# First taps of a feed-forward unit by seven, queued beside products of the next unit by seven

## What is computed

```python
n2 = _rms(h, norm_ffn_w[l])
up = _causal_dwconv(n2 @ w_up[l], ffn_dw_w[l], ffn_dw_b[l])   # 3 taps over the positions
gate, val = jnp.split(up, 2, axis=-1)                          # 2816 channels each
h = h + (jax.nn.silu(gate) * val) @ w_down[l]
```

## Time and profile before

| | |
|---|---|
| median of 3 runs | 1819.34 us |
| the profiled execution | 1819.85 us |
| its span, first to last instruction | 1818.1 us |
| granted TensorE clock | 0.999 |
| TensorE busy | 1795.2 us (99%) |
| VectorE busy | 1390.7 us (76%) |
| ScalarE busy | 964.0 us (53%) |
| GpSimd busy | 154.3 us (8%) |
| feed-forward part, about | 547 to 908 us of the span |

### The profile page before, as it was taken

One profiled execution on the slowest core, in us unless ns is written; L12 is line 12 of the kernel. 1 busy time (PEld: TensorE's weight loads), 2 busy tenths in 40 slices (PEclk: granted clock), 3 DMA queues, 4 the chain that ended last, 5 costly groups with the idle time before them and its releaser, 6 DMA issues.

```text
span 1818.1 us, 32992 instructions
## 1 busy us (share of the span) xinstructions
PE 1795.2 (99%) x13654; PEld 1711.6 (94%) x13654; DVE 1390.7 (76%) x2436; ACT 964.0 (53%) x1874; POOL 154.3 (8%) x130
## 2 busy tenths in 40 slices
PE   9999999999999999999999999999999999999998
PEld 8999999978899989899899999999899999999987
DVE  5888897678756778857889797978358888787844
ACT  6222333568734446536556665666337566666632
POOL 0000000000000011010002121211000111111000
PEclk9999999999999999999999999999999999999999
DMA  5222222200222166454347776765332677777431
GB/s 196 94 85 78 93 94 70 94 24 27 68 76 93 60 167 144 118 138 109 115 117 149 160 160 149 162 152 131 118 93 76 130 156 156 156 152 158 115 123 70
DMA packets 245444, 210.35 MB, mean 116 GB/s; under 512 B 6454, under 2 KB 241775, under 8 KB 245294
## 3 DMA queue, kind: packets, MB, share of 16 engines
q1 hardware_dynamic: 182974, 177.29, 31.7%
q0 software_dynamic: 62304, 30.94, 13.8%
q10 hardware_dynamic: 16, 0.00, 0.0%
HBM read 206.11 MB, written 2.10 MB: 115 GB/s over the span
## 4 chain that ended last, share of the span: by engine, by line
PE 84%; DVE 8%; ACT 6%; issue 1%; DMA 1%; SPq 0%; DVEq 0%; ACTq 0%
PE ps L195 55%; PE ps L199 27%; DVE wlo L210 2%; PE ps L204 2%; ACT whi L207 1%; ACT p L207 1%; DMA s1t<-in_w_up_dram 1%; ACT y L207 1%; DVE raw L210 1%; DVE ast L1135 0%; DVE y L218 0%; ACT zr L207 0%; ACT sw L207 0%; DVE nf L218 0%; DVE mxl L210 0%
## 5 line engine op out<-in xcount | busy, mean ns | idle before, releaser
L210 DVE TENSOR_TENSOR wlo<-raw,whi 128x1024 fp32r<-128x1024 f32 (+1 forms) x359 | 434.8, 1216 | 207.1 <-ACT whi L207 205.5
L207 ACT ACTIVATE whi<-raw 128x1024 fp32r<-128x1024 f32 (+1 forms) x359 | 376.5, 1051 | 239.5 <-PE ps L195 189.3
L195 PE MATMUL ps<-nhi,whi 128*128 128x256 f32 (+3 forms) x1520 | 341.9, 290 | 2.6 <-DVE clo L210 0.8
L195 PE MATMUL ps<-nhi,wlo 128*128 128x256 f32 (+3 forms) x1520 | 337.9, 287 | 0.0
L195 PE MATMUL ps<-nlo,whi 128*128 128x256 f32 (+2 forms) x1392 | 300.7, 287 | 0.0
L195 PEld LDWEIGHTS ps<-nhi,whi 128*128 128x128 f32 x1520 | 246.8, 189 | 6.7 <-DVE clo L210 1.0
L195 PEld LDWEIGHTS ps<-nhi,wlo 128*128 128x128 f32 x1520 | 246.1, 189 | 2.1
L199 PE MATMUL ps<-thi,whi 128*128 128x256 f32 x784 | 224.8, 287 | 1.4 <-DVE wlo L210 0.8
L195 PEld LDWEIGHTS ps<-nlo,whi 128*128 128x128 f32 x1392 | 221.4, 189 | 1.9
L199 PE MATMUL ps<-thi,wlo 128*128 128x256 f32 x784 | 221.6, 283 | 0.0
L199 PE MATMUL ps<-tlo,whi 128*128 128x256 f32 x784 | 221.4, 282 | 0.0
(11 more groups left out here) (342 smaller groups left out, 3514.3 us busy)
## 6 DMA issues: line engine op xcount, KB each, us to landing
raw<-in_w_in_dram SPq DMA_DIRECT2D x90, 1024.0 KB, 5.8
raw<-in_w_up_dram SPq DMA_DIRECT2D x22, 1024.0 KB, 5.4
raw<-in_w_out_dram SPq DMA_DIRECT2D x20, 1024.0 KB, 5.0
s1t<-in_w_in_dram SPq DMA_DIRECT2D x49, 256.0 KB, 2.8
s1t<-in_w_in_dram POOLq DMA_DIRECT2D x49, 256.0 KB, 7.2
raw<-in_w_in_dram POOLq DMA_DIRECT2D x49, 256.0 KB, 4.7
raw<-in_w_down_dram SPq DMA_DIRECT2D x16, 512.0 KB, 3.4
raw<-in_w_conv_out_dram SPq DMA_DIRECT2D x4, 1024.0 KB, 5.0
```

The costliest lines, as they stand in the source:

```text
L195: return pe.put(after, lambda e: e.matmul(o, w, m, start=start, stop=stop_), mark)
L207: return ac.put(after, lambda e: e.activation(o, i, func, **kw))
L210: return dv.put(after, lambda e: e.tensor_tensor(o, a, b, op))
```

## The change

- `seven` loses its parameter `half`: no first tap is queued ahead of product 7.
- `up_seven` gets a parameter `carry` and puts its two first taps (with the entries in `later` that belong to them) on a list `begins`. If another unit by seven of the same group follows directly, they stay there; otherwise both are queued after hook 6.
- If `begins` holds taps, hook 1 and hook 5 of the next unit by seven queue one each, and `step()` is called at hooks 3 and 6 in place of 2 and 5. Otherwise the steps stay at 2 and 5.
- In `up_taps` for tiles with `scaled[0]`, `step()` comes before the first tap in place of behind it.

```diff
--- before.py
+++ after.py
@@ -561,7 +561,7 @@
             for _ in range(min(n, len(loose))):
                 loose.pop(0)()
 
-        def seven(dst, banks, after, hook, direct, summed_, used, width=256, half=None):
+        def seven(dst, banks, after, hook, direct, summed_, used, width=256):
 
 
             s0 = taken[0]
@@ -612,8 +612,6 @@
             c12 = tt([t, u2], d12, C, d12, ALU.add)
             release(c12, banks[2])
             hook(5)
-            if half:
-                half([c11, c12])
             t = used[3] = product(A, dh[:, :, right], dl[:, :, right], td, summed_(3), False, True, u3)
             done(t, s0 + 3)
             c21 = act([t, c22], d21, A, ACT.Copy, scale=-1.0)
@@ -1469,25 +1467,38 @@
                 up_taps(n, a, j, atok, jl, Y[n], lambda i: ZR[n][:, i:i + T2])
                 loose_run(2 if scaled[0] else 1)
 
-            def up_seven(j, atok, jl, banks):
+            begins = []
+
+            def begin(n=2):
+                for _ in range(min(n, len(begins))):
+                    begins.pop(0)()
+
+            def up_seven(j, atok, jl, banks, carry):
+
 
                 ns = [next_y(), next_y()]
+                begins_due = bool(begins)
 
                 def hook(m):
                     tick(1)
-                    if m in (2, 5):
+                    if m in (1, 5):
+                        begin(1)
+                    if m in ((3, 6) if begins_due else (2, 5)):
                         step()
-
-                def taps_of(c, t):
-                    z = ZR[ns[c]].rearrange("p (h t) -> p h t", h=2)
-                    up_taps(ns[c], t, j + c, atok, jl + c, Y[ns[c]].rearrange("p (h t) -> p h t", h=2), lambda i: z[:, :, i:i + 256], False)
 
                 t = seven([ZR[n] for n in ns], banks, [zr_used[n] for n in ns], hook,
                           lambda r, c: (NHI[:, 4 * r:4 * r + 4, SPAN[c]], NLO[:, 4 * r:4 * r + 4, SPAN[c]], ntok[4 * r:4 * r + 4]),
-                          lambda i: (SHI[i], SLO[i], [stok[i]] * 4), [None] * 4, 258, lambda t: taps_of(0, t))
-                taps_of(1, t[1])
+                          lambda i: (SHI[i], SLO[i], [stok[i]] * 4), [None] * 4, width=258)
+                for c, n in enumerate(ns):
+                    z = ZR[n].rearrange("p (h t) -> p h t", h=2)
+                    begins.append(lambda c=c, n=n, z=z: up_taps(n, t[c], j + c, atok, jl + c, Y[n].rearrange("p (h t) -> p h t", h=2),
+                                                                lambda i: z[:, :, i:i + 256], False))
+                if not carry:
+                    begin()
 
             def up_taps(n, ready_, j, atok, jl, y, z, steps=True):
+                if steps and scaled[0]:
+                    step()
                 b = act([ready_, t_vec, y_used[n]], y, z(0), ACT.Identity, bias=cf[:, 132 + j:133 + j], scale=cf[:, j:j + 1])
 
                 def taps():
@@ -1513,7 +1524,7 @@
                         d = tt([up["h", j]], ALO[:, jl, :], AF[:, jl, :], AHI[:, jl, :].bitcast(F), ALU.subtract)
                         atok[jl] = [up["h", j], d]
 
-                if steps:
+                if steps and not scaled[0]:
                     step()
                 later.append([taps, meet, high, rest])
 
@@ -1637,13 +1648,13 @@
                         zs = two_tiles(([pair_dst(TQ), pair_dst(TQ)], HALVES), NHI, NLO, ntok)
                         ffn_stats()
                     elif j in GATES_BY_SEVEN:
-                        up_seven(2 * j, atok, 2 * (j - ja), [6, 7, 4])
+                        up_seven(2 * j, atok, 2 * (j - ja), [6, 7, 4], j in VALUES_BY_SEVEN)
                     else:
                         for c in range(2):
                             z = tile(TQ, NHI, NLO, ntok)
                             up_out(*z, 2 * j + c, atok, 2 * (j - ja) + c)
                     if j in VALUES_BY_SEVEN:
-                        up_seven(NFF + 2 * j, atok, 2 * (j - ja), [5, 2, 3])
+                        up_seven(NFF + 2 * j, atok, 2 * (j - ja), [5, 2, 3], j + 1 < jb)
                     for c in range(2) if j not in VALUES_BY_SEVEN else ():
                         v = tile(TQ, NHI, NLO, ntok)
                         if j == 0 and c == 0:
```

## The result

The changed kernel takes **1813.41 us** (median of 7 runs, 1812.09 to 1814.40), the kernel before 1819.40 in the same comparison (7 runs, 1819.12 to 1821.83): a ratio of 0.9964, 95% interval 0.9952 to 0.9975, so 6.0 us faster where 5.5 were forecast (1813.8 in 1812.6 to 1816.0). A second comparison on another occasion gave 1813.95 against 1819.53, so 5.6 us, ratio 0.9970 (0.9960 to 0.9981).

A forecast was written before the change was run, and what follows sets the result against it. TensorE, busy 99% of the span, was taken as the bound, so only its idle places could yield time. -6.0 us at five late products and +0.5 at G7 gave -5.5, from 1819.34 to 1813.8 us, range 1812.6 to 1816.0.

The forecast's parts named there:

- five late products: Product 3 in V5, G6, V7, V9 and G10, waiting for ScalarE's copy-out of bank A; 6.0 us with restarts.
- Parts 1 to 3: Five unit boundaries: moving first taps away saves 6.0 us; SiLU entering two boundaries and taps at hooks 1, 5 cost nothing.
- One sign: At unit boundaries, `c21` was to start 0.2 us after product 7 instead of waiting for VectorE.
- Part 4: VectorE in V5 and G6: 20.28 us of work in 20.2; cost 0, bounds 0 and +0.2 per unit pair.
- Part 5: Tile units, step before first tap: one more `ahi` ahead of G7's `s1` costs +0.5 us, bounds 0 and 0.7.
- Part 6: In G7 an `alo` moves ahead of the splits for V7's product 3: cover 0.3 us, cost 0, bound +0.3.
- Part 7: G4, G8 and the ends of V7, G6, G10: taps after the last hook cost nothing, cover several us.
- rival (b): Time given back: TensorE reaches each down stage 2 to 3 us earlier and waits there; about 1819 us, chance 0.06.
- Rival (c): Slower: the first tap at hook 1 waits for VectorE, delaying product 5 at five places; 1823 us, chance 0.05.
- Rival (d): Table change around each SiLU that loses its neighbour: price 0 by rows, 1822 by the skill's 2.7 us each; chance 0.01.

## Why the prediction was right, point by point

*What bounds.* Right: TensorE's five late products were the place, and the gain came from there. Their 5.63 and the 0.4 behind them went entirely.

*Parts 1 to 3.* The sums made from one start to the next held to 0.1: `s1` of G6 at E+1.95 (709.29 less 707.34; forecast 1.94), and product 3 was due 0.42 after its release (forecast 0.43); c0 in V5 at E+4.11 and `u2` at E+4.82 (forecast 4.05 and 4.75). One sign did not come at G7/V7, where `c21` waited for VectorE's `c22` and started at E+0.45, not E+0.20; it cost nothing, since `s1` came at E+1.68, and 1.64 was forecast. The run with both taps at the end shows that queue time and wait are two terms: 0.48 remains at V5 with the wait gone, 0.46 was worked out. That the steps are not what gains is shown by the two runs that take them apart.

*Part 4.* Right to take 0, but by a count that was too high. It laid the 20.28 us of VectorE's work in V5 and G6 against 20.2 of time; in the changed kernel the two units hold 9.61 and 9.02, 18.63 in 20.16, as stages come a step later and fall in part behind G6. The run with added work shows how far it was from a bound: 0.6 more per unit cost 0.3 us in all by the trace (0.21 and a slow restart, at V7).

*Part 5, mis-sized.* "For G5 and G9 the sum before `s1` is the same" was the step that failed. The instructions were the same, but not their sum: 0.15 less at each of G5, G7 and G9, because a tap no longer stands directly behind the copy that it reads; the run with the order alone shows it. G7 therefore came 0.60 late, not 0.75, and G5 and G9 0.08, not 0.23. The direction at G7 was right: the `ahi` that moved there costs its 0.52, and the run that takes a tap from there gets the stop back. With 0.45 more the forecast becomes -5.95; the stretch G5 to G10 shows -6.2 (0.11 of the rest lies between the end of V7 and the start of G8), the medians -6.0. The total came out near because the one mis-sized term is small, and not because two errors met.

*Part 6.* V7's split ended at 742.05 and product 3 was due at 742.50, so 0.45 ahead; the forecast's own times (746.0 and 746.46) give the same. With 0.6 of VectorE's work added, product 3 was 0.21 late and began 0.05 after the split's end. So the release takes 0.05 and the cover was 0.40, where the forecast had 0.3.

*Part 7 and rival (b).* No new stop in the down stages or behind; from the end of G10 to the end of the span both traces take 965.6 us, so nothing is given back.

*Rival (c)* took one microsecond for each microsecond of stop. It did not come: c0 waited for nothing in V5 (701.37, straight behind the split). Whether its price was right no run shows. At its threshold the stops are 1.8 us each; behind those of 1.58 and 2.09 no slow stretch followed, behind those of 2.32 and more one may, and then a stop costs some 1.5 us on top.

*Rival (d).* A SiLU alone between a split and a copy (708.77 to 709.29) takes its 0.52 without idle time. The trace of the changed kernel agrees with the rows of before, and not with a change of tables there.

## What to carry to other kernels

When TensorE waits at one instruction for one small copy, list everything that stands ahead of this copy in its engine's queue since the last product, with the wait of the first; here a tap that VectorE took up only 6.4 us after it was ready (700.09 and 706.47) waited for another engine and held two evacuations behind it. Move such work to a hook where its input is old and the next evacuation is not due. And lay the order so that an instruction does not stand directly behind the one whose output it reads, if an independent one can go between.

## What the runs showed of the hardware that was not expected

- On ScalarE an instruction that waits for the one just ahead of it, to read its output or for its end alone, starts 0.14 us later than an independent one: 0.64 and 0.50 behind a copy of 128x514 (here it reads), 0.66 and 0.52 behind an instruction of 128x512 (here it only waits).
- After a stop of TensorE in the feed-forward part its granted clock fell to 0.50 for 3.4 us (once 6.8) in some cases and stayed at 1.00 in others, with the same kernel and the same stop; 3.4 us of it cost about 1.5. It did so behind seven of ten stops of 2.32 to 3.56 us, and behind none of the two of 2.09 or the shorter ones. The Trainium skill, "TensorE: Matmul & The Clock Gate", section "HAM oscillation — how this bites in real kernels", tells of the clock falling when TensorE has long idle gaps; the traces agree, but they show it behind gaps mostly shorter than those that the page tells of, and coming and going with the execution. They also show a stretch at 0.50 at 9 to 10 us of the span in eight of twelve traces, beside a stop of at most 0.9 us, and one in attention in three of twelve, at a place that has no stop above 0.9 us in the 40 us ahead of it. What decides there stays open.
- VectorE at 99% of a stretch cost TensorE nothing, as long as each split had its cover.
